# First mixer of a fp32 decoder trunk: gate and drive products from VectorE to GpSimd, and three orders of the work in its attention steps

## The chip, the cores and the metric

One core of one Trainium2 chip. The time is device microseconds of one execution; three executions of the kernel before took 1423.74, 1423.98 and 1425.97 us, median 1423.98.

## The reference

Two decoder layers on 512 tokens of width 1024, all in fp32. Each layer is a mixer, cross-attention to 256 memory tokens and a SwiGLU block, each behind an RMS norm. The change touches the mixer of layer 0 alone, which is

```python
proj = h @ w_in
x_br, y_br, q, k, v = jnp.split(proj, list(AB_SPLITS), axis=-1)
rec = rg_lru(causal_depthwise_conv(x_br, conv_w, conv_b), wa, ba, wx, bx, lam) * jax.nn.gelu(y_br)
...
att = dilated_attention(q, k, heads(v))
return jnp.concatenate([rec, att], axis=-1) @ w_out
```

and inside `rg_lru`

```python
r = jax.nn.sigmoid(block_diag_linear(x, wa, ba)); i = jax.nn.sigmoid(block_diag_linear(x, wx, bx))
log_a = -LRU_C * r * jax.nn.softplus(-lam); a = jnp.exp(log_a)
u = jnp.sqrt(-jnp.expm1(2.0 * log_a)) * (i * x)
h_t = a_t * h_{t-1} + u_t
```

`i * x` is the gate product, the product with the square root is the drive. Eight heads of width 64 attend over the 512 tokens.

## The kernel before

Activations stand transposed: 8 tiles of 128 channels x 512 tokens. Every matrix product is fp32 by three matmuls (`product`, L556, L559, L560): high part of the weight by high part of the activation, high by low, low by high. Weights arrive in **units** of 128x1024 values, 226 in the whole program, through a ring of 4 slots:

- SP issues the DMA of unit u once TensorE has begun unit u - 3 (`unit`, a wait on `s_used`);
- GpSimd makes its high part, `w_hi` (`high_part`, L512);
- VectorE subtracts to get the low part, `w_lo` (`low_part`, L1007), which overwrites the raw weights;
- TensorE waits for the low part and runs the 24 matmuls of 512 columns of the unit.

Each engine has one instruction stream, written out by hand; what stands behind a waiting instruction on its engine waits too. Nothing is reordered. `low_to(u)` on VectorE and `high(u0, u1)` on GpSimd issue all low (high) parts up to a unit at that place.

The first mixer in order: units in_x (8), in_q (4), gates (4, one per 256 channels), in_k (4), in_v (4), y0 to y7 (the branch for GeLU), 4 units for the memory's keys, and out0 (2 groups of 6). The mixer's own units are numbered from `mx_unit`; its units 0 to 7 are y0 to y7, 8 to 11 the memory's keys, and 12 onwards belong to out0.

**The recurrence.** ScalarE takes two sigmoids per tile from PSUM (`lru_r`, L1662, and `gate_i`, L1665). VectorE forms `xc = gate_i * xc` (`gated`, L1263), between the rotations of q (`qk_tile`, L1079 to L1082) and low parts. ScalarE makes the decay `lru_a` and the square root (`s_ls`). VectorE's `recur` forms the drive `lru_r * xc` (L1285) and runs the scan over the tokens (L1286), tile by tile, with the rotations of k and the low parts of in_v 3 and of y0 to y2 between. Then come the maxima of the attention's step 0 (L1331).

**The attention steps.** Twelve steps s = 0 to 11 compute scores, three steps for each pair of heads. TensorE's step is: values of an earlier pair, transposes of earlier probabilities (`mixer_turns`, L849), scores (L833), then a unit of weights (`y_half(s)` for s < 8, memory keys for s < 12, then units of out0 at s = 12 to 16). Scores of step s wait for the maxima of step s - 1. `y_half` with odd s completes two y tiles in PSUM; VectorE multiplies them by the norm (`y_tile`, L1292), and the first matmul of the next y tile in that bank waits for it (`s_y`). VectorE's step is written out in this loop:

```python
if s < STEPS + 2:
    low_to(mx_unit + s + 3)
if s in (1, 3, 5, 7):
    y_tile(s - 1)
```

preceded by the copies of transposed probabilities (L1347), the maxima, at s = 3, 6, 9, 12 the reciprocals of the denominators (L1339), the low part of a head output (`mixer_output`, L1352) and `rec`, the product with GeLU (L1296). STEPS is 12. GpSimd at s = 3, 6, 9, 12 normalises both heads of the pair, four instructions each (`normalise_pair`, L504), and at every step makes one high part, behind them. After the loop VectorE waits for the last head output and `residual` issues the low parts still missing.

## Time and profile before

| what | value |
|---|---|
| median of three runs | 1423.98 us |
| the profiled execution | 1420.2 us, span 1418.4 us |
| TensorE busy | 1349.2 us, 95% |
| VectorE busy | 771.0 us, 54% |
| ScalarE busy | 356.3 us, 25% |
| GpSimd busy | 313.3 us, 22% |
| DMA | 127.18 MB, mean 90 GB/s |

Busy shares are over the whole span; a matmul's end is modelled, so TensorE's share is an upper reading. The profile names engines PE (TensorE), PEld (its weight loads), DVE (VectorE), ACT (ScalarE), POOL (GpSimd) and SP. In a timeline row a bracket gives the idle time before the instruction and what ended it; "x2" says that two equal instructions are merged, and a length then spans both.

### The profile page before, as it was taken

How to read it: one execution, taken by the hardware profiler on the slowest of the kernel's cores; microseconds unless marked ns; L12 is line 12 of the kernel's file. 1: busy time of each engine (PE TensorE's matmuls, PEld its weight loads, DVE VectorE, ACT ScalarE, POOL GpSimd, SP SyncE). 2: the span in 40 equal slices, each digit the busy share in tenths (PEclk: the TensorE clock that was granted, in tenths of full speed). 3: DMA queues.
4: the chain of work that ended last, by engine and by line, in shares of the span. 5: the costliest groups of instructions: out<-in, count | busy, mean ns of one | idle time of the engine just before them, and what ended most of it. 6: DMA issues, size and time to landing. Idle time of an engine off the chain costs nothing.

```text
span 1418.4 us, 17415 instructions
## 1 busy us (share of the span) xinstructions
PE 1349.2 (95%) x6440; PEld 1104.4 (78%) x6440; DVE 771.0 (54%) x1147; ACT 356.3 (25%) x730; POOL 313.3 (22%) x358
## 2 busy tenths in 40 slices
PE   8999799999899999999999986799899999999997
PEld 7888577788678888888888875688678888888886
DVE  6997856436475443344436867438475443344434
ACT  4338255212342110001112235513331110001113
POOL 2222123312321212121212124312321121212120
PEclk9999899999999999999999997899999999999999
DMA  5333222222223332323233320022223332333321
GB/s 197 99 102 89 60 75 75 68 96 89 89 90 98 95 100 93 102 91 103 89 104 89 104 90 16 1 89 90 71 79 103 91 102 94 100 95 98 97 95 74
DMA packets 92418, 127.18 MB, mean 90 GB/s; under 512 B 5568, under 2 KB 58048, under 8 KB 92352
## 3 DMA queue, kind: packets, MB, share of 16 engines
q1 hardware_dynamic: 92352, 126.27, 28.0%
q8 instruction: 45, 0.74, 0.2%
q14 instruction: 21, 0.17, 0.0%
HBM read 124.15 MB, written 2.10 MB: 89 GB/s over the span
## 4 chain that ended last, share of the span: by engine, by line
PE 76%; DVE 9%; issue 6%; POOL 4%; DMA 3%; ACT 1%; SPq 0%; DVEq 0%; POOLq 0%; ACTq 0%
PE ps L556 24%; PE ps L560 24%; PE ps L559 24%; DVE w_lo L1007 2%; POOL w_hi L512 2%; DVE acc L1028 1%; DVE prob_attn L1122 1%; DMA raw<-in_w_in 1%; DMA raw<-in_xa_wkv 1%; DVE h L1047 1%; POOL prob_xattn L493 1%; POOL prob_attn L493 1%; PE ps L692 1%; DVE xc L1286 1%; POOL prob_mixer L504 1%
## 5 line engine op out<-in xcount | busy, mean ns | idle before, releaser
L1007 DVE TENSOR_TENSOR w_lo<-raw,w_hi 128x1024 fp32r<-128x1024 f32 x226 | 283.0, 1253 | 466.5 <-POOL w_hi L512 464.9
L512 POOL TENSOR_SCALAR w_hi<-raw 128x1024 fp32r<-128x1024 f32 x226 | 247.8, 1097 | 966.3 <-DMA raw<-in_w_gate_up 410.5
L556 PE MATMUL ps<-z_hi,w_hi 128*128 128x512 f32 x1040 | 409.8, 394 | 7.1 <-DVEq L1050 2.9
L560 PE MATMUL ps<-z_hi,w_lo 128*128 128x512 f32 x1040 | 405.8, 390 | 0.0
L559 PE MATMUL ps<-z_lo,w_hi 128*128 128x512 f32 x1040 | 405.6, 390 | 0.0
L556 PE MATMUL ps<-f_hi,w_hi 128*128 128x512 f32 x608 | 240.6, 396 | 3.9 <-DVE w_lo L1007 2.8
L556 PEld LDWEIGHTS ps<-z_hi,w_hi 128*128 128x128 f32 x1040 | 195.9, 188 | 54.5 <-issue 6.1
L560 PE MATMUL ps<-f_hi,w_lo 128*128 128x512 f32 x608 | 238.0, 391 | 0.0
L559 PE MATMUL ps<-f_lo,w_hi 128*128 128x512 f32 x608 | 237.9, 391 | 0.0
L559 PEld LDWEIGHTS ps<-z_lo,w_hi 128*128 128x128 f32 x1040 | 196.0, 188 | 41.8 <-issue 1.4
L560 PEld LDWEIGHTS ps<-z_hi,w_lo 128*128 128x128 f32 x1040 | 195.7, 188 | 41.0
L556 PEld LDWEIGHTS ps<-f_hi,w_hi 128*128 128x128 f32 x608 | 115.0, 189 | 29.2 <-DVE w_lo L1007 3.0
L559 PEld LDWEIGHTS ps<-f_lo,w_hi 128*128 128x128 f32 x608 | 115.0, 189 | 24.6 <-issue 1.0
L560 PEld LDWEIGHTS ps<-f_hi,w_lo 128*128 128x128 f32 x608 | 115.0, 189 | 24.3
L1769 ACT ACTIVATE ff_g<-ff_g 128x512 f32<-128x512 f32 x44 | 27.8, 632 | 347.0 <-DVE ff_g L1464 346.9
L1772 ACT ACTIVATE f_hi<-ff_u 128x512 f32 (+1 forms) x44 | 27.2, 633 | 183.4 <-DVE ff_u L1475 183.4
L1514 ACT ACTIVATE z_hi<-h,vec 128x512 fp32r<-128x512 f32 x48 | 34.8, 724 | 142.5 <-DVEq L1052 141.4
L1537 ACT ACTIVATE sq<-h 128x512 f32<-128x512 f32 x56 | 35.2, 629 | 49.0 <-DVEq L1052 23.3
L1047 DVE TENSOR_TENSOR h<-ps,h 128x512 f32<-128x512 f32 x56 | 38.5, 688 | 12.5 <-PE ps L560 11.6
L1022 DVE SCALAR_TENSOR_TENSOR z_lo<-h,vec,z_hi 128x512 fp32r<-128x512 f32 x48 | 39.6, 826 | 9.1 <-DVE h L1047 6.9
L1464 DVE TENSOR_TENSOR ff_g<-ps,rstd 128x512 f32<-128x512 f32 x44 | 30.3, 692 | 22.2 <-PE ps L560 22.1
L493 POOL TENSOR_SCALAR prob_attn<-prob_attn,stat 128x128 f32<-128x128 f32 (+1 forms) x64 | 31.7, 515 | 43.9 <-DVE stat L1137 43.9
(205 smaller groups left out, 1189.5 us busy)
## 6 DMA issues: line engine op xcount, KB each, us to landing
raw<-in_w_gate_up SPq DMA_DIRECT2D x176, 256.0 KB
raw<-in_w_down SPq DMA_DIRECT2D x44, 512.0 KB
raw<-in_w_in SPq DMA_DIRECT2D x20, 512.0 KB
raw<-in_w_out SPq DMA_DIRECT2D x20, 512.0 KB
raw<-in_xa_wkv SPq DMA_DIRECT2D x16, 512.0 KB
raw<-in_w_in SPq DMA_DIRECT2D x16, 256.0 KB
raw<-in_xa_wq SPq DMA_DIRECT2D x8, 512.0 KB
raw<-in_xa_wo SPq DMA_DIRECT2D x8, 512.0 KB
```

Of the source, the lines that this page charges most:

```text
L493: ins = pool.tensor_scalar(a["prob"][n % 3][:, c:c + w], a["prob"][n % 3][:, c:c + w], stat[:, n % 3, 4, i:i + 1], 1.0, ALU.mult, ALU.mult)
L512: pool.tensor_scalar(w_hi[:, slot], raw[:, slot], 1.0, 1.0, ALU.mult, ALU.mult).then_inc(s_hi, 1)
L556: ins = pe.matmul(o, whi, rhi, start=start, stop=False)
L559: pe.matmul(o, whi, rlo, start=False, stop=False)
L560: return pe.matmul(o, wlo, rhi, start=False, stop=stop)
L1007: dve.tensor_tensor(w_lo[:, slot], raw[:, slot], w_hi[:, slot].bitcast(F32), ALU.subtract).then_inc(s_lo, 1)
L1022: dve.scalar_tensor_tensor(z_lo[:, m, :], h[:, m, :], v(f"g_{norm}", m), z_hi[:, m, :].bitcast(F32), ALU.mult, ALU.subtract).then_inc(s_zl, 1)
L1047: ins = dve.tensor_tensor(h[:, m, :], ps[:, b, :], h[:, m, :], ALU.add)
L1464: dve.tensor_tensor(ff_g[:, p, :], ps[:, b0 + p, :], rstd[:], ALU.mult).then_inc(s_ff_gate, 1)
L1514: act.activation(dst[:, m, :], h[:, m, :], ACT.Identity, scale=v(f"g_{norm}", m)).then_inc(s_zh, 1)
L1537: act.activation(sq[:, m % 2, :], h[:, m, :], ACT.Square).then_inc(s_sq, 1)
L1769: act.activation(ff_g[:, p, :], ff_g[:, p, :], ACT.Silu).then_inc(s_ff_silu, 1)
```

## The change

- The eight gate products and the eight drive products are issued by GpSimd (`gated`, `driven`), with the same operands. ScalarE's waits on `s_gx` are unchanged; VectorE's scan waits for the new semaphore `s_drive` in place of `s_ls`.
- GpSimd's high parts of in_k, in_v and the first y units are issued between these products at written-out places.
- `normalise_pair` makes the step's high part between the first and the second head.
- On VectorE the y tile of an odd step comes ahead of that step's low part, and the low parts are issued in the loop for two steps more (s < STEPS + 4).

```diff
--- before.py
+++ after.py
@@ -272,7 +272,7 @@
         s_xch, s_xcl = sem("s_conv_hi"), sem("s_conv_lo")
         s_y_done, s_y, s_yg = sem("s_y_done"), sem("s_y_scaled"), sem("s_gelu")
         s_sp_e, s_sp = sem("s_exp_lambda"), sem("s_softplus")
-        s_gate, s_gx = sem("s_gate_i"), sem("s_gated_input")
+        s_gate, s_gx, s_drive = sem("s_gate_i"), sem("s_gated_input"), sem("s_drive")
         s_at, s_lq, s_ls = sem("s_decay"), sem("s_one_minus_a2"), sem("s_input_scale")
         s_rec, s_rech, s_recl = sem("s_rec"), sem("s_rec_hi"), sem("s_rec_lo")
         s_q0, s_v0 = sem("s_qk0"), sem("s_v0")
@@ -494,10 +494,12 @@
                                              stat[:, n % 3, 4, i:i + 1], 1.0, ALU.mult, ALU.mult)
                 ins.then_inc(a["s_prob"], 1)
 
-            def normalise_pair(p):
+            def normalise_pair(p, unit):
 
                 pool.wait_ge(mx["s_rden"], p + 1)
                 for e in range(2):
+                    if e:
+                        high(unit, unit + 1)
                     prob = mx["prob"][2 * p + e]
                     for i in range(TB):
                         c, w = mx["start"][i], P * (i + 1)
@@ -525,12 +527,34 @@
                     high_part(u, u % SLOTS)
 
             at_unit = 0
+            def gated(m):
+
+                pool.wait_ge(s_gate, m + 1)
+                pool.tensor_tensor(xc[:, m, :], gate_i[:, m % 2, :], xc[:, m, :], ALU.mult).then_inc(s_gx, 1)
+
+            def driven(m):
+
+                pool.wait_ge(s_ls, m + 1)
+                pool.tensor_tensor(lru_r[:, m, :], lru_r[:, m, :], xc[:, m, :], ALU.mult).then_inc(s_drive, 1)
+
+            first = UNIT0["gates"]
+            high(at_unit, first + 4)
+            for m in range(DB):
+                gated(m)
+                if m % 2:
+                    high(first + 4 + m // 2, first + 5 + m // 2)
+            high(first + 8, first + 11)
+            for m in range(DB):
+                driven(m)
+                if m in (5, 7):
+                    high(first + 6 + m - (m == 7), first + 7 + m - (m == 7))
             first = UNIT0["mixer"]
-            high(at_unit, first + 2)
+            high(first + 1, first + 2)
             for s in range(STEPS + 2):
                 if s % 3 == 0 and s:
-                    normalise_pair(s // 3 - 1)
-                high(first + s + 2, first + s + 3)
+                    normalise_pair(s // 3 - 1, first + s + 2)
+                else:
+                    high(first + s + 2, first + s + 3)
             at_unit = first + STEPS + 4
             for name in ("xattn0", "attn1", "xattn1"):
                 first = UNIT0[name]
@@ -1258,19 +1282,10 @@
                     dve.wait_ge(s_q0, t)
                 rotate(x_[:, n, :], x_[:, n, :], rope0, s_q0, cos_r, sin_r)
 
-            def gated(m):
-                dve.wait_ge(s_gate, m + 1)
-                dve.tensor_tensor(xc[:, m, :], gate_i[:, m % 2, :], xc[:, m, :], ALU.mult).then_inc(s_gx, 1)
-
             gates0 = UNIT0["gates"]
             for t in range(4):
                 qk_tile(t)
-                if t:
-                    gated(2 * t - 2)
-                    gated(2 * t - 1)
                 low_to(gates0 + 3 + t)
-            gated(6)
-            gated(7)
             low_to(gates0 + 7)
 
             def decay(m):
@@ -1281,8 +1296,7 @@
 
             def recur(m):
 
-                dve.wait_ge(s_ls, m + 1)
-                link(dve.tensor_tensor(lru_r[:, m, :], lru_r[:, m, :], xc[:, m, :], ALU.mult))
+                dve.wait_ge(s_drive, m + 1)
                 link(dve.tensor_tensor_scan(xc[:, m, :], lru_a[:, m, :], lru_r[:, m, :], 0.0, ALU.mult, ALU.add))
 
             def y_tile(m):
@@ -1378,10 +1392,10 @@
                 if s in (STEPS, STEPS + 1):
                     for m in range(4 * (s - STEPS), 4 * (s - STEPS) + 4):
                         rec_low(m)
-                if s < STEPS + 2:
-                    low_to(mx_unit + s + 3)
                 if s in (1, 3, 5, 7):
                     y_tile(s - 1)
+                if s < STEPS + 4:
+                    low_to(mx_unit + s + 3)
             dve.wait_ge(mx["s_o_lo"], 4)
             dve.nop().then_inc(s_free[(GROUP0["mixer"] + 1) % 2], 4)
             residual("xa0", s_done["out0"], group0=GROUP0["out0"], units=(UNIT0["out0"] + 6, UNIT0["xq0"]))
```

GpSimd from the gates to the first pair of heads, before (line 512 makes a high part, 504 normalises):

```order
L512 TENSOR_SCALAR w_hi<-raw 128x1024 x4
L374 REGISTER_ALU
L374 COMPARE_AND_BRANCH
L512 TENSOR_SCALAR w_hi<-raw 128x1024 x5
L504 TENSOR_SCALAR prob_mixer_127<-prob_mixer_127,stat_107 128x128
L504 TENSOR_SCALAR prob_mixer_127<-prob_mixer_127,stat_107 128x256
L504 TENSOR_SCALAR prob_mixer_127<-prob_mixer_127,stat_107 128x384
L504 TENSOR_SCALAR prob_mixer_127<-prob_mixer_127,stat_107 128x512
```

and now (533 is a gate product, 538 a drive product, 514 a high part, 506 normalises):

```order
L533 TENSOR_TENSOR xc<-gate_i,xc 128x512 x2
L514 TENSOR_SCALAR w_hi<-raw 128x1024
L533 TENSOR_TENSOR xc<-gate_i,xc 128x512 x2
L514 TENSOR_SCALAR w_hi<-raw 128x1024
L533 TENSOR_TENSOR xc<-gate_i,xc 128x512 x2
L514 TENSOR_SCALAR w_hi<-raw 128x1024
L533 TENSOR_TENSOR xc<-gate_i,xc 128x512 x2
L514 TENSOR_SCALAR w_hi<-raw 128x1024 x4
L538 TENSOR_TENSOR lru_r<-lru_r,xc 128x512 x6
L514 TENSOR_SCALAR w_hi<-raw 128x1024
L538 TENSOR_TENSOR lru_r<-lru_r,xc 128x512 x2
L514 TENSOR_SCALAR w_hi<-raw 128x1024 x5
```

The products stand in front of high parts of in_k (first three pairs), between in_k and in_v, and six of the drive products ahead of in_v 3.

VectorE at step 3 of the attention, before, from the reciprocals of the first pair:

```order
L1339 RECIPROCAL stat_107<-stat_107 128x8
L1007 TENSOR_TENSOR w_lo<-raw,w_hi 128x1024
L1292 TENSOR_TENSOR y_in<-ps,rstd 128x512 x2
L1347 COPY prob_t_mixer_135<-ps 128x384
L1331 ISA prob_mixer_129,stat_107<-ps,m_82 128x384
```

and now (line 1353 is the reciprocal, 1031 a low part, 1306 a y tile):

```order
L1353 RECIPROCAL stat_107<-stat_107 128x8
L1306 TENSOR_TENSOR y_in<-ps,rstd 128x512
L1031 TENSOR_TENSOR w_lo<-raw,w_hi 128x1024
L1306 TENSOR_TENSOR y_in<-ps,rstd 128x512
L1361 COPY prob_t_mixer_135<-ps 128x384
L1345 ISA prob_mixer_129,stat_107<-ps,m_82 128x384
```

The two y tiles stood together behind the low part; now one is ahead of it and one behind, and the copy of the transposed probabilities follows.

VectorE at the end of the steps, before (1300 is a recurrence tile's low part, 1352 a head output's low part, 1047 a residual tile of out0):

```order
L1300 TENSOR_TENSOR f_lo<-xc,f_hi 128x512 x4
L1007 TENSOR_TENSOR w_lo<-raw,w_hi 128x1024
L1347 COPY prob_t_mixer_142<-ps 128x384
L1352 TENSOR_TENSOR f_lo<-ps,f_hi 128x512 x2
L1007 TENSOR_TENSOR w_lo<-raw,w_hi 128x1024 x5
L1047 TENSOR_TENSOR h<-ps,h 128x512
```

and now (1314, 1366 and 1071 are the same three):

```order
L1314 TENSOR_TENSOR f_lo<-xc,f_hi 128x512 x4
L1031 TENSOR_TENSOR w_lo<-raw,w_hi 128x1024
L1361 COPY prob_t_mixer_142<-ps 128x384
L1366 TENSOR_TENSOR f_lo<-ps,f_hi 128x512
L1031 TENSOR_TENSOR w_lo<-raw,w_hi 128x1024 x2
L1366 TENSOR_TENSOR f_lo<-ps,f_hi 128x512
L1031 TENSOR_TENSOR w_lo<-raw,w_hi 128x1024 x3
L1071 TENSOR_TENSOR h<-ps,h 128x512
```

Two low parts of weights stand between the last two head outputs; before, all five came behind the last one.

## Rows read from the trace of the kernel before

**Rows 1.** the page: the chain that ended last, by engine, and the costliest GpSimd group
```profile
PE 76%; DVE 9%; issue 6%; POOL 4%; DMA 3%; ACT 1%; SPq 0%; DVEq 0%; POOLq 0%; ACTq 0%
...
L512 POOL TENSOR_SCALAR w_hi<-raw 128x1024 fp32r<-128x1024 f32 x226 | 247.8, 1097 | 966.3 <-DMA raw<-in_w_gate_up 410.5
```

**Rows 2.** TensorE by stretch: stretch and length, busy (instructions), granted clock, DMA share, GB/s
```profile
109.70:160.00 50.30, 50.26 (x224) 1.00 0.32 95
160.00:168.70 8.70, 0.10 (x1) 0.62 0.00 0
168.70:172.50 3.80, 3.79 (x10) 0.52 0.10 10
...
191.70:194.10 2.40, 0.13 (x3) 1.00 0.01 3
281.00:285.00 4.00, 4.00 (x11) 0.57 0.34 131
```

**Rows 3.** who waited for whom, 160 to 169 us; groups by form, 80 to 280 us
```profile
PE ps L833 <- DVE stat L1331: 8.6, 1, 8.6
...
L1263 DVE TENSOR_TENSOR xc<-gate_i,xc 128x512 f32<-128x512 f32 x8 | 7.0, 901 | 1.5 <-ACT gate_i L1665 1.5
```

**Rows 4.** VectorE in order of time, 131 to 169 us: start, length, instruction
```profile
131.55 1.23 DVE L1007 TENSOR_TENSOR w_lo<-raw,w_hi 128x1024 fp32r<-128x1024 f32 x1 [1.88 <-POOL w_hi L512]
...
141.28 1.95 DVE L1007 TENSOR_TENSOR w_lo<-raw,w_hi 128x1024 fp32r<-128x1024 f32 x1
143.16 0.74 DVE L1079 STREAM_SHUFFLE rope<-k 128x512 f32<-128x512 f32 x1
...
149.35 1.22 DVE L1007 TENSOR_TENSOR w_lo<-raw,w_hi 128x1024 fp32r<-128x1024 f32 x1
...
168.23 0.42 DVE L1331 CUSTOM_DVE_ANT_0 prob_mixer<-ps,m 128x256 f32<-128x256 f32 x1
```

**Rows 5.** VectorE and GpSimd where both read SBUF, and GpSimd's 128x512 alone
```profile
134.66 0.69 DVE L1285 TENSOR_TENSOR lru_r<-lru_r,xc 128x512 f32<-128x512 f32 x1
135.39 1.23 DVE L1286 TENSOR_TENSOR_SCAN xc<-lru_a,lru_r 128x512 f32<-128x512 f32 x1
135.80 1.66 POOL L512 TENSOR_SCALAR w_hi<-raw 128x1024 fp32r<-128x1024 f32 x1 [4.29 <-DMA raw<-in_w_in]
136.65 1.35 DVE L1285 TENSOR_TENSOR lru_r<-lru_r,xc 128x512 f32<-128x512 f32 x1
...
191.24 2.05 DVE L1007 TENSOR_TENSOR w_lo<-raw,w_hi 128x1024 fp32r<-128x1024 f32 x1 [5.26 <-POOL w_hi L512]
...
235.45 0.69 POOL L504 TENSOR_SCALAR prob_mixer<-prob_mixer,stat 128x512 f32<-128x512 f32 x1
```

**Rows 6.** the stops of TensorE at 192, 241 and 248 us and what stands before them
```profile
184.52 0.50 PE L556 MATMUL ps<-z_hi,w_hi 128*128 128x512 f32 x1
186.07 4.12 POOL L504 TENSOR_SCALAR prob_mixer<-prob_mixer,stat 128x128 f32<-128x128 f32 x8 [10.14 <-DVE stat L1339]
193.21 1.28 DVE L1292 TENSOR_TENSOR y_in<-ps,rstd 128x512 f32<-128x512 f32 x2
194.03 0.47 PE L556 MATMUL ps<-z_hi,w_hi 128*128 128x512 f32 x1 [2.27 <-DVE y_in L1292]
...
239.23 2.06 DVE L1007 TENSOR_TENSOR w_lo<-raw,w_hi 128x1024 fp32r<-128x1024 f32 x1 [5.26 <-POOL w_hi L512]
241.81 0.98 PE L849 MATMUL ps<-ident,prob_mixer 128*128 128x128 f32 x7 [0.84 <-DVE prob_t_mixer L1347]
...
248.87 0.50 PE L556 MATMUL ps<-f_hi,w_hi 128*128 128x512 f32 x1 [1.15 <-DVEq L1372]
```

**Rows 7.** the end of the mixer, 268 to 281 us, three engines
```profile
268.09 1.05 POOL L512 TENSOR_SCALAR w_hi<-raw 128x1024 fp32r<-128x1024 f32 x1 [5.19 <-DMA raw<-in_w_out]
...
278.74 0.69 DVE L1352 TENSOR_TENSOR f_lo<-ps,f_hi 128x512 fp32r<-128x512 f32 x1 [13.54 <-ACT f_hi L1721]
...
280.86 0.50 PE L556 MATMUL ps<-f_hi,w_hi 128*128 128x512 f32 x1 [2.79 <-DVE w_lo L1007]
```

## The prediction

> **What bounds the kernel now.** I read the chain that ended last first: 76% of it is TensorE, 9% VectorE, 6% issue, 4% GpSimd [rows 1]. So time can be won only where TensorE stands still or is slow, and only in the first mixer, which alone is edited. The table of stretches shows where that is [rows 2]. From 109.7 to 160.0 us TensorE is busy 50.26 of 50.30 us: nothing that other engines do late there costs anything as yet. From 160.0 to 168.7 it does nothing. Three shorter stops follow, of 2.27, 0.84 and 1.15 us before the matmuls at 194.03, 241.81 and 248.87 [rows 6], and one of 2.79 us before 280.86 [rows 7]. The clock comes on top: from 168.7 to 172.5 TensorE had 0.52 of its clock, from 281.0 to 285.0 it had 0.57, so mostly the lower of its two levels (1.2 of 2.4 GHz), after stops of 8.6 and 2.8 us; around the stop of 2.27 us it kept 1.00 [rows 2].
>
> Then, for each stop, who ended it. The long one is ended by a statistic of VectorE (L1331), 8.6 us [rows 3]: the maxima of step 0, which end at 168.65 (168.23 + 0.42) [rows 4]. VectorE reaches them at the end of one unbroken piece of work that begins at 131.55, when the high part of unit in_v 2 is there: low parts, the eight recurrences, four rotations of k. So a microsecond off this piece is a microsecond off the stop, up to 8.6. The stop at 191.7 is ended by y_in at 193.21+, which stands in VectorE's order behind a low part; that one waited for GpSimd, whose order was: eight normalising instructions (186.07 to 190.19), then the high part [rows 6]. At 239.23 the same pattern. The stop at 278.1 is ended by the low part of unit 16 of the mixer (out0's fifth), which VectorE issues only behind the last head output, f_lo at 278.74 [rows 7]; the high part of the unit after it had been made at 268.09.
>
> **The change, part by part.**
>
> *Gate products on GpSimd (8).* They leave VectorE between 93 and 110 us (7.0 us busy [rows 3]) and are issued by GpSimd between high parts. They may delay the high parts of in_k by a product or two; the cover is the stretch 109.7 to 160 in which TensorE never waits [rows 2]. GpSimd has room: it stood idle 966 us ahead of high parts [rows 1]. Cost and gain nil. If the cover failed, the price would be one wait of a product's length at the start of in_k.
>
> *Drive products on GpSimd (8).* This is the disputed part. VectorE loses eight products, each 0.73 us from its start to its scan's (134.66 to 135.39 [rows 5]): 8 x 0.73 = 5.8 us, all in the piece that sets the long stop. But now each scan waits for GpSimd's product, behind which stand GpSimd's high parts of in_v 3 (asked for by the low part at 141.28 [rows 4], hence VectorE waits for products 4 and 5 too) and y0 to y2. What matters is whether a product runs beside VectorE. The rows say no: GpSimd's high part at 135.80 took 1.66 us while a scan ran until 136.62, and the VectorE product asked for at 136.65 took 1.35 instead of 0.69, until the high part was over; the low part at 191.24 took 2.05 against 1.22 for that at 149.35 [rows 4, 5]. Instructions of the two engines that both read SBUF take turns, whole instruction by whole instruction. So a product moved to GpSimd still costs VectorE's chain its length.
>
> Its length is in no row. Lower end: GpSimd's one-input operation on the same 128x512, 0.69 us [rows 5]. A high part moves 128x1024 in, as many elements as the two inputs of a product, and takes 1.05 undisturbed (268.09 [rows 7]; mean of all 226, waits included, 1.097 [rows 1]). Upper end: twice that, 2.1. I take 1.05, since the number of elements read is the same.
> - eight products: 8 x 1.05 = +8.4
> - taken off VectorE: -5.8
> - one product beside a shuffle of 0.74, which reads one tile [rows 4]: -0.7
> - a GpSimd instruction that has stood waiting ended 0.84 after the scan, not 1.05 (136.62 to 137.46) [rows 5]; about five of eight wait so: -1.0
> - sum: **+0.9 us**; at the lower end 5.5 - 5.8 - 1.7 = -2.0, at the upper 16.8 - 5.8 - 1.7 = +9.3.
>
> So the largest edit should win nothing: the long stop and the slow clock behind it stay. The low part of y0, done at 150.57 before [rows 4], gets some 5 us later and makes TensorE wait about a microsecond at 154.4; this only moves idle time forward, since TensorE would wait for the maxima anyway.
>
> The Trainium skill (SBUF — State Buffer, Who interferes with whom) says that a VectorE instruction with two SBUF inputs and a GpSimd one that reads SBUF exclude each other for the whole instruction; by that rule the trace agrees (1.35 for 0.69). The Trainium skill (GPSIMD Engine Reference, Elementwise — side-by-side cycle accounting) speaks against the move: 4497 ns for a two-input operation on 2048 elements, so 1.12 us for 512 as an estimate, with which the sum would be +1.5; no row here has a product on GpSimd.
>
> *y tiles ahead of low parts, step 3.* y_in of tile 2 needs only the first half of y_half(3), which began at 184.52 [rows 6]: 12 of its matmuls at the pace of 224 in 50.3 us [rows 2] are 2.7 us, so 187.2; VectorE is free since 186.0, when GpSimd begins to normalise. So it is ready at 188 and tile 3 at about 191, before TensorE needs them at 191.76 (194.03 less 2.27) and half a unit later. **-2.3 us** [rows 6]. Behind it, the low part of that step comes at about 189.2 instead of 191.24: the high part now follows four normalisings (half of 4.12 us) instead of eight. Late next: the second head's probabilities, by 1.05 us plus a low part's turn, until about 192.3; TensorE turns them at step 5, after 197. Covered. At steps 1, 5 and 7 the low part waits for a y tile that follows half a unit; it is needed a unit later or more.
>
> *High part between heads, steps 6, 9, 12.* At step 9 the low part starts some 2 us before its 239.23, by half of such a normalising. VectorE's copy, maxima and low parts follow 2 us earlier; the 0.84 us stop at 241.81 goes, and of the 1.15 before 248.87 some 0.4, since there memory_keys itself must end before mk is copied. **-1.2 us** (ends: -0.8 if only the first goes, -2.0 if both). At step 6 TensorE did not wait; at step 12 neither.
>
> *Low parts at steps 14 and 15 (the bound is now STEPS + 4).* Units 16 and 17 get their low parts at about 265 and 270, behind high parts of which the second is there at 269.1 [rows 7] and the first a step earlier. The last two turns of TensorE's steps then don't wait: **-2.8 us** [rows 7], and without that stop the clock should not fall: 4.0 us at 0.57 would be 2.3, **-1.7 us** [rows 2]. Late next: f_lo of the last head, 279.43, wanted only by unit 17, 5.5 us later. Covered.
>
> No DMA is added; SP's waits are on TensorE's progress and move with it.
>
> Sum: 0.9 - 2.3 - 1.2 - 2.8 - 1.7 = **-7.1 us**. The profiled execution took 1420.2 us (span 1418.4), so 1413.1 for such a one. The median of the runs is 3.8 us above it; I take the difference over to it: 1423.98 - 7.1 = 1416.9. A measurement of this kernel can tell about 0.2% (2.8 us) from no change.
>
> **The rivals.**
>
> *The products do run beside VectorE.* Then 5.8 us come off the chain, the long stop shrinks to 2.8, and the slow clock (3.8 us at 0.52, 1.8 us) may go or stay, since 2.79 brought it and 2.27 did not: -5.8 - 0.9 - 8.0 = -14.7, 1409.3. For it: no two-input GpSimd operation has been seen. Against: the turns in [rows 5]. 12%.
>
> *The stops won later come back.* The microseconds of the y tiles and heads meet the next wait (scores behind maxima, copies behind turned heads), and only the end of the mixer is won: 0.9 - 2.8 - 1.7 = -3.6, 1420.4. For it: behind the maxima the exponentials, GeLU and the recurrence's product follow one another on two engines before the next low part. Against: VectorE was idle 5.26 us just ahead of the low parts at 191.24 and 239.23 [rows 5, 6]. 18%.
>
> *The product is dear (the other side).* Each scan waits for one, and taking turns puts every microsecond of eight products into the 131 to 168 piece. The late gains of 8.0 are eaten when the product takes 0.9 + 8 (p - 1.05) = 8.0, p = 1.94; at the upper end of 2.1 the time is 1425.3, and at 2.5 it is 1428.5. From 2.3 on it is measurably slower. For it: GpSimd's per-element work with two inputs is unseen. Against: one-input work runs at 1.0 ns an element. 10%.
>
> **How the numbers follow.** Forecast 60%, with its own range 1413 (product 0.69, both small stops) to 1422.6 (product 1.5, clock still falls). The range of 8 in 10 takes in most of the first rival: 1408 to 1423. Faster by over 0.2% (below 1421.1): 57 of the 60, the 12, and half of the 18: 0.78. Within: 0.14. Slower: the worse part of the last rival, 0.08.
>
> **What would show it.** Right: product on GpSimd near 1.05 to 1.25 us and longer when a scan runs; the stop before step 1's scores still 8 to 10 us, with a granted clock near half after it; no stop for y_in near 192; full clock through out0. Wrong: that stop shrunk below 4 us (products overlap) or grown past 14 (dear product); a new stop of over 1 us between 190 and 250; a fall of the clock in out0; any part of the kernel after 300 us that changes by more than the profile repeats.

## The result and the profile after

The change runs in 1415.64 us (median of 6 runs, 1411.88 to 1418.62), the kernel before beside it in 1423.06 (6 runs, 1418.67 to 1425.97). The ratio is 0.9948, with a 95% interval of 0.9924 to 0.9972: 7.4 us less, between 4.0 and 10.8. A second set of 5 runs gave 0.9952 [0.9939, 0.9966], 6.8 us less. The forecast was 7.1 less, 1416.9.

The profiled execution of the change took 1417.91 us (span 1416.1), only 2.3 us below the profiled one of before. The profiled one of before was a quick execution (1420.2 beside a median of 1423.06), and the two profiles differ in places that the change doesn't touch; how much of each difference is the change's is worked out below by stretches.

The page of the change: busy time by engine, and the chain that ended last.

```profile
PE 1348.0 (95%) x6440; PEld 1103.1 (78%) x6440; DVE 777.5 (55%) x1131; ACT 356.1 (25%) x730; POOL 348.1 (25%) x374
...
PE 78%; DVE 8%; issue 6%; POOL 4%; DMA 2%; ACT 1%; SPq 0%; DVEq 0%; POOLq 0%; ACTq 0%
```

TensorE's share of the chain went from 76 to 78%, VectorE's from 9 to 8% [rows 1]. Sixteen instructions left VectorE and came to GpSimd. What they cost there stands in the groups of GpSimd by form, 80 to 170 us (busy us, mean ns; idle time before), and in the shortest, median and longest drive product:

```profile
L538 POOL TENSOR_TENSOR lru_r<-lru_r,xc 128x512 f32<-128x512 f32 x8 | 15.7, 2000 | 0.0
L533 POOL TENSOR_TENSOR xc<-gate_i,xc 128x512 f32<-128x512 f32 x8 | 13.8, 1744 | 3.0 <-ACT gate_i L1679 3.0
```

```profile
L538 POOL TENSOR_TENSOR lru_r<-lru_r,xc x8: 1285/2213/2291, 131.5 to 146.0; 128x512 f32<-128x512 f32 x8
```

A product undisturbed takes 1.285 us. The usual one takes 2.2, most of it spent waiting for a scan to end. VectorE in order of time shows the same from the other side (start, length, instruction, idle time before):

```profile
131.60 2.30 DVE L1031 TENSOR_TENSOR w_lo<-raw,w_hi 128x1024 fp32r<-128x1024 f32 x1 [1.61 <-POOL w_hi L514]
133.83 8.84 DVE L1300 TENSOR_TENSOR_SCAN xc<-lru_a,lru_r 128x512 f32<-128x512 f32 x4
144.87 2.23 DVE L1031 TENSOR_TENSOR w_lo<-raw,w_hi 128x1024 fp32r<-128x1024 f32 x1 [2.21 <-POOL w_hi L514]
...
148.73 1.52 DVE L1105 TENSOR_TENSOR rope<-rope,sin_r 128x512 f32<-128x512 f32 x1
150.29 1.42 DVE L1106 TENSOR_TENSOR k<-rope,rope 128x512 f32<-128x512 f32 x1
...
154.98 1.22 DVE L1031 TENSOR_TENSOR w_lo<-raw,w_hi 128x1024 fp32r<-128x1024 f32 x1
156.12 4.99 DVE L1300 TENSOR_TENSOR_SCAN xc<-lru_a,lru_r 128x512 f32<-128x512 f32 x4
...
170.44 0.42 DVE L1345 CUSTOM_DVE_ANT_0 prob_mixer<-ps,m 128x256 f32<-128x256 f32 x1
```

The first four scans take 8.84 us, the last four, with no product beside them, 4.99. One scan, the product issued while it ran, and the next scan:

```profile
136.19 2.14 DVE L1300 TENSOR_TENSOR_SCAN xc<-lru_a,lru_r 128x512 f32<-128x512 f32 x1
137.20 2.22 POOL L538 TENSOR_TENSOR lru_r<-lru_r,xc 128x512 f32<-128x512 f32 x1
...
138.36 2.14 DVE L1300 TENSOR_TENSOR_SCAN xc<-lru_a,lru_r 128x512 f32<-128x512 f32 x1
```

They end at 138.33, 139.42 and 140.50, each some 1.09 us behind the one before. So the two engines take turns, as in [rows 5], but not for the whole of an instruction: a scan and a product together take 2.17 us where one after the other would be 1.23 + 1.285 = 2.52, so 0.35 us of each pair is hidden.

The piece from the low part of in_v 2 to the maxima of step 0 was 37.10 us (131.55 to 168.65, [rows 4]) and is 39.26 now (131.60 to 170.86): +2.2. VectorE issues eight instructions fewer in it and ends later. By the starts in both profiles, the second four scans with what belonged to them are 3.6 us shorter, since their products were ready; the first four are 0.2 longer; the low part at 131.60 costs 1.1 more (2.30 instead of 1.23, [rows 4]) and that at 144.87 0.3; VectorE stands idle 2.2 us ahead of the latter, whose high part GpSimd makes behind six products; and the first two rotations of k take 1.8 more (steps of 1.52 and 1.42 instead of 0.69), beside high parts that the products have pushed back. The Trainium skill (SBUF — State Buffer, Who interferes with whom) has the two engines exclude each other for the whole instruction. Here that holds for all but the 0.35 us of a pair.

TensorE's stops in the change, in order of time (start, length, matmul, idle time before and what ended it):

```profile
109.84 0.50 PE L580 MATMUL ps<-z_hi,w_hi 128*128 128x512 f32 x1 [0.83 <-ACTq L1682]
...
156.25 0.60 PE L580 MATMUL ps<-z_hi,w_hi 128*128 128x512 f32 x1 [1.75 <-DVE w_lo L1031]
...
170.92 1.65 PE L857 MATMUL ps<-k,q 64*128 64x384 f32 x4 [7.31 <-DVE stat L1345]
...
248.28 0.50 PE L580 MATMUL ps<-f_hi,w_hi 128*128 128x512 f32 x1 [0.65 <-DVEq L1386]
```

Of the stops in [rows 6] those at 194.03 and 241.81 have no counterpart, that at 248.87 is down from 1.15 to 0.65, and that at 280.86 [rows 7] is gone: the mixer's last matmuls run straight into its unit 16 at 277.41. New is the one before 156.25, for the low part of y0. The table of TensorE's stretches of the change (stretch and length, busy, granted clock, DMA share, GB/s) answers [rows 2]:

```profile
109.80:156.20 46.40, 44.67 (x200) 1.00 0.31 91
156.30:161.00 4.70, 4.70 (x14) 0.64 0.37 113
...
171.00:175.00 4.00, 4.00 (x10) 0.50 0.13 18
...
191.00:260.00 69.00, 68.30 (x467) 1.00 0.24 77
260.00:300.00 40.00, 40.00 (x213) 1.00 0.24 82
```

From 260 to 300 us TensorE was busy 40.00 of 40.00 us at the full clock; before it was 37.21 of 40.00:

```profile
260.00:300.00 40.00, 37.21 (x194) 0.96 0.22 76
```

**The stretches.** Three marks divide the mixer, each the start of a matmul: in_k's first, step 1's first scores (behind the long stop), out0's first unit; a fourth is the first stop of the cross-attention behind it. The lengths between them, worked out from the starts in each profile (us), take out what differed before 109 us and behind 370 us:

```
kernel                         in_k to    scores    out0 to   in_k to
                               scores     to out0   attention attention
before [rows 6]                 58.97      80.16     119.71    258.84
before, second profile          59.05      80.78     119.75    259.58
change                          61.08      77.36     115.26    253.70
change, second profile          61.13      76.86     115.24    253.23
products back on VectorE        59.24      76.59     115.25    251.08
products alone                  61.10      82.77     119.67    263.54
gate products alone, with rest  59.32      76.78     115.26    251.36
y tile order alone              58.64      78.82     119.66    257.12
head order alone                59.08      77.40     118.09    254.57
low bound alone                 60.87      80.73     115.25    256.85
drive with one input            55.74      77.56     115.27    248.57
```

The change against before, by the means of two profiles each: +2.1, -3.4, -4.5, together -5.7. The predicted terms were +0.9 for the first, -3.5 (2.3 and 1.2) for the second, -4.5 (2.8 and 1.7) for the third.

### The profile page after: what moved, and what is told of

Same layout as the page of the kernel before. It is cut to its first block, busy times and chain, and to the rows that moved or that the text cites. A ratio compares the mean times of both kernels' runs of the same rounds, so it can differ in the third digit from the quotient of the medians.

```text
span 1416.1 us, 17405 instructions
## 1 busy us (share of the span) xinstructions
PE 1348.0 (95%) x6440; PEld 1103.1 (78%) x6440; DVE 777.5 (55%) x1131; ACT 356.1 (25%) x730; POOL 348.1 (25%) x374
## 4 chain that ended last, share of the span: by engine, by line
PE 78%; DVE 8%; issue 6%; POOL 4%; DMA 2%; ACT 1%; SPq 0%; DVEq 0%; POOLq 0%; ACTq 0%
PE ps L580 25%; PE ps L583 24%; PE ps L584 24%; DVE w_lo L1031 1%; POOL w_hi L514 1%; DVE acc L1052 1%; DVE prob_attn L1146 1%; DVE h L1071 1%; PE ps L716 1%; DMA raw<-in_xa_wkv 1%; POOL lru_r L538 1%; POOL prob_xattn L493 1%; POOL prob_attn L493 1%; PE ps L684 1%; DVE z_lo L1046 1%
## 5 line engine op out<-in xcount | busy, mean ns | idle before, releaser
L514 POOL TENSOR_SCALAR w_hi<-raw 128x1024 fp32r<-128x1024 f32 x226 | 251.4, 1112 | 926.2 <-DMA raw<-in_w_gate_up 411.5
L1783 ACT ACTIVATE ff_g<-ff_g 128x512 f32<-128x512 f32 x44 | 27.8, 632 | 348.2 <-DVE ff_g L1478 348.2
```

Source lines behind the costliest of these rows:

```text
L514: pool.tensor_scalar(w_hi[:, slot], raw[:, slot], 1.0, 1.0, ALU.mult, ALU.mult).then_inc(s_hi, 1)
L1783: act.activation(ff_g[:, p, :], ff_g[:, p, :], ACT.Silu).then_inc(s_ff_silu, 1)
```

## The experiments

Each kernel was timed beside the kernel before on one chip; ratios have their 95% interval. In microseconds they are taken on that set's median of before (1424.22, 1422.6 and 1424.36).

**1. Both products back on VectorE; all that the change does later is kept.**

```diff
-                dve.wait_ge(s_drive, m + 1)
+                dve.wait_ge(s_ls, m + 1)
+                link(dve.tensor_tensor(lru_r[:, m, :], lru_r[:, m, :], xc[:, m, :], ALU.mult))
...
+                if t:
+                    gated(2 * t - 2)
+                    gated(2 * t - 1)
```

> The change without its first part: gate and drive products back on VectorE, the head order, y tile order and the two further low parts kept. Theory A (a GpSimd product and VectorE's scans take turns at SBUF, so the products cost): the scores of step 1 start near 168.7 us as before (170.9 in the change), the stop of 1.75 us before the first y unit and the low clock behind it go, and the time is 2.5 to 3.5 us below the change, about 10 us below before. Rival B (the products are neutral): same as the change, 7 us below before. Rival C (they help): slower than the change.

Measured: 1415.03 us, 0.9933 [0.9917, 0.9950], 9.5 us less than before. In its profile the first stretch is back at 59.2 and the other two are the change's. So the later parts carry the whole gain, and the products give a part of it back: 2.4 us by the length from in_k to the attention (253.5, the mean of the change's two profiles, against 251.1), 2.1 to 2.7 by the ratios, which were taken on different chips and whose intervals overlap.

**2. The products alone, on the kernel before.**

```diff
-            def gated(m):
-                dve.wait_ge(s_gate, m + 1)
-                dve.tensor_tensor(xc[:, m, :], gate_i[:, m % 2, :], xc[:, m, :], ALU.mult).then_inc(s_gx, 1)
...
+            def driven(m):
+                pool.wait_ge(s_ls, m + 1)
+                pool.tensor_tensor(lru_r[:, m, :], lru_r[:, m, :], xc[:, m, :], ALU.mult).then_inc(s_drive, 1)
```

> The kernel before with only the sixteen products moved to GpSimd. Theory A: the scores of step 1 at about 171 us, a new stop of 1 to 2 us before the first y unit, and a time 2.5 to 3.5 us above before. Rival B: no difference. Rival C: several us below before, with the stop before step 1 shrunk from 8.6 towards 3 us.

Measured: 1423.59 us (12 runs), 0.9992 [0.9981, 1.0002]: no change that can be told. The first stretch is 61.10, as in the change. The stop for the low part of y0 is there too, and the y_in stop stays. TensorE's stops in it:

```profile
155.73 0.79 PE L577 MATMUL ps<-z_hi,w_hi 128*128 128x512 f32 x1 [1.77 <-DVE w_lo L1028]
...
170.39 1.65 PE L854 MATMUL ps<-k,q 64*128 64x384 f32 x4 [7.32 <-DVE stat L1342]
...
196.69 0.76 PE L577 MATMUL ps<-z_hi,w_hi 128*128 128x512 f32 x1 [2.24 <-DVE y_in L1303]
```

The expectation of 2.5 to 3.5 us above before failed. The first stretch alone would make this kernel 2.1 us slower, and the other half of this edit, the gate products, gives some 0.8 back (experiment 4). That leaves +1.3, and the interval of the runs ends at +0.3: the last microsecond stays open. The profile can't tell, since it is that of the slowest of the 12 executions (1427.17 us), and its long middle stretch (82.77) has a slower clock behind the y_in stop, which neither profile of before has:

```profile
196.69:203.00 6.31, 6.31 (x21) 0.73 0.28 86
```

**3. The drive product with one input.** Each drive product is an operation of the same size with one input, so the product with xc is left out of the computation.

```diff
-                pool.tensor_tensor(lru_r[:, m, :], lru_r[:, m, :], xc[:, m, :], ALU.mult).then_inc(s_drive, 1)
+                pool.tensor_scalar(lru_r[:, m, :], lru_r[:, m, :], 1.0, 1.0, ALU.mult, ALU.mult).then_inc(s_drive, 1)
```

> The changed kernel with the drive product on GpSimd replaced by a one-input copy of the same 128x512 shape (the product with xc is left out of the computation). Theory A (the length of the product sits in VectorE's chain, 1.29 us against 0.69): eight times 0.6 us come off, the scores of step 1 start near 166 us instead of 170.9. Rival D (what costs is the hand-over between the engines, a wait per scan, not the length): they start at 170 or later.

Measured: 1411.01 us, 0.9898 [0.9881, 0.9914]. Its drive line (shortest, median, longest) and the long stop:

```profile
L538 POOL TENSOR_SCALAR lru_r<-lru_r x8: 615/1516/1586, 130.6 to 140.3; 128x512 f32<-128x512 f32 x8
```

```profile
164.66 1.65 PE L857 MATMUL ps<-k,q 64*128 64x384 f32 x4 [5.40 <-DVE stat L1345]
```

Undisturbed, the operation is 0.67 us shorter (615 against 1285 ns). Eight times that is 5.4, and the first stretch is 5.3 shorter than the change's (55.74 against 61.08). So a microsecond more of a product on GpSimd is a microsecond more of VectorE's chain, as the prediction's formula had it, and no mere cost of handing over. The hidden part is the same in both: here a scan and an operation take 1.48 us (1.23 + 0.615 = 1.85 one after the other). (The timed distance to the change, by the ratios of two chips, is 7.7 us; the 2.4 beyond the first stretch are not found in the profiles.)

**4. The gate products on GpSimd, the drive products on VectorE**, beside the change and the kernel before once more, on the same chip.

```diff
-            high(first + 8, first + 11)
-            for m in range(DB):
-                driven(m)
-                if m in (5, 7):
-                    high(first + 6 + m - (m == 7), first + 7 + m - (m == 7))
+            high(first + 8, first + 13)
...
-                dve.wait_ge(s_drive, m + 1)
+                dve.wait_ge(s_ls, m + 1)
+                link(dve.tensor_tensor(lru_r[:, m, :], lru_r[:, m, :], xc[:, m, :], ALU.mult))
```

> The changed kernel with the drive products back on VectorE and the gate products left on GpSimd. Theory G (the gate products on GpSimd help: on VectorE they hold up ScalarE's sigmoids, and TensorE starts in_k 2.0 us late instead of 0.83; the drive products cost): stop before in_k at 0.83, scores of step 1 near 168, time 1 to 3 us below both the change and e1. Rival H (gate products neutral): same as e1.

> The changed kernel again, on the same chip as its variants. Every theory: 6 to 9 us below before. Its profile shows whether the stop of 1.75 us before the first y unit, the low clock behind it and the late scores of step 1 (170.9) are steady or chance.

> The kernel before once more, for a second profile. Theory F (the first profile was a lucky one: its median is 4 us above it, and other profiles show 2.10 us instead of 0.70 at the cross-attention and a low clock behind stops of about 2 us): this profile shows at least one of these, or the stop of 2 us instead of 0.83 us before in_k at about 109 us. Rival: the same stops to 0.1 us.

Measured: the gate products alone 1412.96 us, 0.9928 [0.9914, 0.9941]; the change 1415.13, 0.9952 [0.9939, 0.9966]. On one chip, the drive products cost 2.2 us by the medians and 3.4 by the ratios, and by the profiles 1.8 (61.13 against 59.32). All five executions of the one are shorter than all five of the other (at most 1414.17, at least 1414.46).

The second profile of the kernel before brought what the prediction had missed. Its TensorE waited 1.88 us ahead of in_k, where the first profile had 0.83, and ScalarE's rows say why (start, length, instruction; in brackets its wait). TensorE's row follows:

```profile
97.47 0.69 ACT L1665 ACTIVATE gate_i<-ps,vec 128x512 f32<-128x512 f32 x1 [0.16 <-DVE xc L1263]
...
103.23 0.69 ACT L1665 ACTIVATE gate_i<-ps,vec 128x512 f32<-128x512 f32 x1 [0.49 <-DVE xc L1263]
...
109.13 0.69 ACT L1665 ACTIVATE gate_i<-ps,vec 128x512 f32<-128x512 f32 x1 [0.94 <-DVE xc L1263]
```

```profile
111.09 0.50 PE L556 MATMUL ps<-z_hi,w_hi 128*128 128x512 f32 x1 [1.88 <-ACTq L1668]
```

gate_i has two buffers, and ScalarE may fill one only when the product has read it. In this execution VectorE was late with the products, each time by more, and ScalarE handed it on to TensorE. In the first profile of before it was the other way round: VectorE waited for gate_i, 1.5 us in all [rows 3], and the stop was 0.83. Of the seven profiles with the gate products on VectorE five have the long form (1.88 to 2.06 us), two the short one; of the seven with them on GpSimd none has it, all show 0.83. From the first gate_i to in_k's first matmul it is 16.93 us in the short form (92.81 to 109.74) and 17.99 in the long one (93.10 to 111.09). So the gate products on GpSimd save 1.1 us in about five executions of seven, 0.8 on average; in_k's first matmul starts at 110.1 in the mean of the one seven profiles and at 109.0 in that of the other. The runs can't settle it: by the ratios this kernel and experiment 1 are 0.7 us apart (0.9928 and 0.9933), with intervals that overlap. Five of seven is a small count. What decides the form lies ahead of the gates: VectorE began its first rotation of q 7.1 to 7.2 us ahead of the first gate_i in the two short profiles, 3.8 to 4.6 us ahead in the five long ones. What makes it late there stays open.

**5. The y tile ahead of the low part, alone.**

```diff
-                if s < STEPS + 2:
-                    low_to(mx_unit + s + 3)
                 if s in (1, 3, 5, 7):
                     y_tile(s - 1)
+                if s < STEPS + 2:
+                    low_to(mx_unit + s + 3)
```

> The kernel before with only the y tile of an odd step ahead of the low part. Theory A: the stop of 2.2 us before the y unit of step 4 becomes shorter but may not go, since the head order is unchanged and tile 3 still stands behind the low part at 191; 1 to 2.3 us are won, and up to 1.8 more where the low clock followed that stop; all other stops stay. Rival I (the stop moves to the next step): stops in steps 4 to 6 sum to the same.

Measured: 1419.0 us (11 runs), 0.9969 [0.9959, 0.9980], 4.4 less. The stop at 192 is gone; those of 0.83 at 240.68, 1.20 at 247.78 and 2.79 at 279.77 stay. The middle stretch is 1.7 shorter than the mean of before.

**6. The high part between the heads, alone.**

```diff
-            def normalise_pair(p):
+            def normalise_pair(p, unit):
...
+                    if e:
+                        high(unit, unit + 1)
...
-                    normalise_pair(s // 3 - 1)
-                high(first + s + 2, first + s + 3)
+                    normalise_pair(s // 3 - 1, first + s + 2)
+                else:
+                    high(first + s + 2, first + s + 3)
```

> The kernel before with only the step's high part between the two heads. Theory A: the low part of step 3 starts 2 us earlier, so the stop of 2.2 us in step 4 becomes about 0.2, that of 0.8 in step 11 goes and that before out0 shrinks from 1.2 to about 0.7: 2.5 to 3.5 us won. Rival: the second head's probabilities come late and TensorE waits for them in steps 5, 8, 11 or 14.

Measured: 1416.95 us, 0.9956 [0.9941, 0.9972], 6.3 less. This edit alone removes the stop at 241 and the one at 192 too: VectorE in its profile, behind the earlier high part:

```profile
190.12 1.39 DVE L1010 TENSOR_TENSOR w_lo<-raw,w_hi 128x1024 fp32r<-128x1024 f32 x1 [3.21 <-POOL w_hi L514]
191.43 1.28 DVE L1295 TENSOR_TENSOR y_in<-ps,rstd 128x512 f32<-128x512 f32 x2
```

The low part comes 1.1 us earlier and is 0.66 shorter than before (1.39 against 2.05, [rows 5]), since a short normalising instruction runs beside it and not another high part (GpSimd at 190.06 to 190.43 here, at 191.17 to 192.22 before), and y_in starts 1.8 earlier. So the two reorderings earn the same 2.3 us at step 3. The middle stretch is 3.1 shorter here and 1.7 shorter in experiment 5, and with both, in experiment 1, 3.9. Yet experiment 1 has no stop fewer than this kernel between the scores and out0 (one, 0.66 us in both), and its whole lead of 0.8 us is there when step 2's scores start, 8.54 us behind step 1's against 9.35 here. It is the clock behind the long stop, 20 us of it in experiment 1 and then here:

```profile
169.10:189.10 20.00, 20.00 (x81) 0.89 0.26 79
```

```profile
168.51:188.51 20.00, 20.00 (x77) 0.85 0.24 70
```

The second profile of before had 0.87 there, that of experiment 5 had 0.86. So the y tile order adds nothing to the head order.

The end of the mixer holds a lesson on the clock. This kernel still has the stop of 2.79 us:

```profile
277.90 0.50 PE L559 MATMUL ps<-f_hi,w_hi 128*128 128x512 f32 x1 [2.79 <-DVE w_lo L1010]
```

```profile
260.00:300.00 40.00, 37.21 (x201) 1.00 0.24 79
```

Behind the same stop the clock stayed at 1.00, where both profiles of before show 0.96 over these 40 us. The third stretch is 118.09 instead of 119.7: 1.6 us, which is the predicted price of the clock (1.7) by itself. Of the five profiles with this stop it is the only one that kept the clock.

**7. The low parts of two more steps in the loop, alone.**

```diff
-                if s < STEPS + 2:
+                if s < STEPS + 4:
                     low_to(mx_unit + s + 3)
```

> The kernel before with only the two further low parts in the loop (units 16 and 17 at steps 14 and 15). Theory A: the stop of 2.79 us before unit 16 and the clock of about 0.57 behind it go, 4.5 us are won (2.8 + 1.7). Rival: the clock stays low for another reason and 2.8 us are won.

Measured: 1416.49 us, 0.9949 [0.9933, 0.9965], 7.3 less. The third stretch is 115.25: 4.5 shorter, the predicted 2.8 and 1.7 to a tenth. The timed gain is larger than that by 2.8, about the half-width of its interval (2.3) and a little more; the profile doesn't show where it would be. Its first stretch is 1.9 longer than before's (60.87), and the part as such has no effect there. It is the long form of the gate stop once more, this time with a slower clock behind it:

```profile
109.50:135.00 25.50, 24.18 (x99) 0.93 0.30 83
```

Seven hundredths of 25.5 us are 1.8, about the 1.9. In the long forms of experiment 1, of experiment 5 and of the second profile of before the clock stayed at 1.00.

**8. The chain of the long stop in another order.** All the above leaves the largest stop where it is: step 1's scores wait for the maxima of step 0, and behind its first four scans VectorE puts four more, four rotations and four low parts ahead of those maxima. In three kernels only one scan, one rotation and two low parts stay ahead of them; the rest is spread over steps 0 to 5: on experiment 1 (products on VectorE), on experiment 4 (gate products on GpSimd), and on the change itself. The edit of the second and third:

```diff
             qk_tile(4)
-            qk_tile(5)
+            recur(4)
             low_to(gates0 + 13)
-            for m in range(4, DB):
-                recur(m)
-            low_to(gates0 + 13)
-            qk_tile(6)
-            low_to(gates0 + 14)
-            qk_tile(7)
             mx_unit = UNIT0["mixer"]
-            low_to(mx_unit + 3)
...
                     mixer_maxima(s)
+                if s == 0:
+                    low_to(mx_unit + 2)
+                    recur(5)
+                    recur(6)
+                if s == 1:
+                    recur(7)
+                if s == 2:
+                    qk_tile(5)
+                if s == 4:
+                    qk_tile(6)
+                if s == 5:
+                    qk_tile(7)
```

The first has qk_tile(5) at step 1, not 2.

> Products on VectorE as in e1, and the long stop attacked itself: on VectorE only the recurrences 0 to 4, one rotation of k and the low part of y0 stand ahead of the maxima of step 0; recurrences 5 to 7 and the other rotations follow in steps 0, 1, 4 and 5. Theory A (the long stop is VectorE's order alone): the 8.6 us stop and the low clock behind it (1.8 us) go, and 8 to 10 us more come off than in e1, so 16 to 20 us below before. Rival E (the moved work only moves the stop to steps 1 to 5): 0 to 4 us below e1.

> e8 with the gate products on GpSimd and the fifth rotation moved from step 1 to step 2. Theory G: stop before in_k 0.83 us instead of 2.06, the stop of 1.40 us before y unit 2 gone, so 2 to 3 us below e8, about 23 us below before. Rival: no difference to e8.

> e10 with the drive products on GpSimd as well, as in the change, but VectorE's new order. Theory A (a product on GpSimd costs only where VectorE's chain sets the end): scans 0 to 4 are late by about 3 us, the low part of the first y unit comes after TensorE wants it, a stop of 1 to 2 us at 154 us and perhaps the low clock behind it remain: 1 to 3 us slower than e10. Rival: no slower, since the chain now has several us to spare.

Measured:

```
products on VectorE        1403.15 us  0.9849 [0.9834, 0.9863]
gate products on GpSimd    1401.61 us  0.9855 [0.9840, 0.9870]
both on GpSimd             1403.93 us  0.9856 [0.9836, 0.9875]
```

All three are 20.5 to 21.5 us faster than the kernel before and 13 to 15 faster than the change. Against the kernels that differ in this edit alone, the reordering wins 12.0 us (experiment 1), 10.4 (experiment 4) and 13 to 14 (the change). In the first one stop is left between in_k and out0, for a y_in that follows the rotation at step 1:

```profile
170.24 0.47 PE L569 MATMUL ps<-z_hi,w_hi 128*128 128x512 f32 x1 [1.40 <-DVE y_in L1305]
```

In the second there is none. Its VectorE now reaches the maxima of step 0 at 153.22 and waits for TensorE there, not the other way round:

```profile
153.22 0.29 DVE L1335 CUSTOM_DVE_ANT_0 prob_mixer<-ps,m 128x128 f32<-128x128 f32 x1 [4.51 <-PE ps L853]
```

```profile
109.00:233.00 124.00, 123.51 (x683) 1.00 0.28 86
```

That is 123.51 of 124.00 us busy at the full clock. From in_k to the attention it takes 240.1 us (108.36 to 348.47), 19.1 less than before and 11.3 less than experiment 4. In the third the drive products on GpSimd leave a stop of 0.32 us at 154.37, and that length is 240.5: where VectorE's chain has slack, the same two microseconds of turns cost 0.4. The runs don't tell these versions apart: the second was expected 2 to 3 us below the first and is not (0.9855 and 0.9849), though its profile is 3.0 shorter from in_k to the attention; the third was expected 1 to 3 above the second and is not either (0.9856), so there the rival held.

## Why the prediction was right

**The sum.** Predicted -7.1, measured -7.4 and -6.8 in two sets of runs. By the stretches and the gate stop: +2.1 - 3.4 - 4.5 - 0.8 = -6.6. Two terms were off, one up and one down, and they nearly cancel: that the sum met the time this well is in part luck. The stretches also leave out a difference behind the third stop of the cross-attention, +1.7 us in the profiles (below), for which the prediction had no term; with it the profiles give -4.9, which is just inside the intervals of both sets.

**Drive products: the mechanism right, the size off.** The prediction took 1.05 us for a product by the number of elements read, between bounds of 0.69 and 2.1; it takes 1.285. Put into its own formula (0.24 more, eight times) the term is +2.8; the profiles show +2.1, and the one-input experiment moves the chain by 5.3 where the lengths say 5.4. The term of -1.0 for waiting products had the right cause: one ended 1.09 us behind the scan, not 1.285. A scan behind a product gains likewise (1.08 instead of 1.23), for which there was no term. And the cost comes in elsewhere than the formula says, mostly as VectorE's wait for the high part behind six products (2.2 us). The estimate worked out from the Trainium skill (GPSIMD Engine Reference, Elementwise — side-by-side cycle accounting), 1.12 us and so +1.5, was nearer than 1.05 and still short of the measured 1.285. That the long stop stays (7.31 and 8.91 us), and that the largest edit wins nothing, was right: alone it measures 0.9992 [0.9981, 1.0002].

**The low part of y0** was to come 5 us later, with a microsecond of waiting at 154.4 that only moves idle time forward. It started 5.6 later (154.98 against 149.35), and the stop was 1.75. It cost nothing, as said: in the second profile of the change the clock kept 1.00 behind it (154 to 163 us), in the first it fell to 0.64, and the scores start 61.1 us behind in_k in both, because the long stop takes up the difference (7.31 and 8.91 us).

**Gate products: the step that failed.** "Cost and gain nil" named TensorE's cover from 109.7 on and GpSimd's idle time, but not who waits for the product in the stretch before: ScalarE, through the two buffers of gate_i, and TensorE behind it. The rows shown [rows 3] had VectorE waiting for gate_i there, and one profile was taken for the rule. It is the rarer of the two forms seen. The term is about -0.8 by the profiles, and more where the slower clock follows the long form, as it did in two of those five (1.8 us each).

**y tiles and heads:** -3.5 predicted for both, -3.9 measured without the products and -3.4 (mean of two) with them. The assignment was off: the head order does not only reach step 9 but also undoes the stop at step 3, so that by the stops it earns all of it alone and the y tile order adds nothing to it (experiment 6); what the stretches differ by beyond that is the clock behind the long stop. No wait came in their place: between 190 and 250 us the one stop is 0.65.

**Low parts at steps 14 and 15:** -4.5 predicted, -4.5 in every profile that has the edit and a full clock. The clock's 1.7 of it is a matter of chance: the head order alone kept the clock behind the same stop.

**The rivals.** That products run beside VectorE is excluded, but for the 0.35 us of a pair, by the turns of scans and products and by the one-input experiment. That the stops won come back is excluded by the middle stretch. The dear product needed 1.94 us and is 1.285.

**After 300 us** the prediction asked for nothing that changes. One thing does: the third stop of the cross-attention is 2.10 us in both profiles of the change and 0.70 and 0.42 in those of before.

```profile
374.08 1.18 PE L699 MATMUL ps<-ident,prob_xattn 128*128 128x128 f32 x8 [2.10 <-POOL prob_xattn L493]
```

```profile
379.14 1.09 PE L675 MATMUL ps<-ident,prob_xattn 128*128 128x128 f32 x8 [0.70 <-POOL prob_xattn L493]
```

The stop itself costs nothing. From the matmul behind the first of the three stops to that behind the third it is 10.5 to 10.6 us in all fourteen profiles. What differs is the clock. Before, it fell behind the second stop, where TensorE then worked longer and waited less, and was full behind the third:

```profile
374.22:377.02 2.80, 2.80 (x10) 0.50 0.01 3
379.12:383.12 4.00, 3.98 (x18) 1.00 0.00 0
```

In the change it held behind the second and fell behind the third, where TensorE works without a pause:

```profile
369.18:371.98 2.80, 2.79 (x12) 1.00 0.01 3
374.08:378.08 4.00, 4.00 (x13) 0.61 0.00 0
```

From there to TensorE's next stop it is 27.8 to 28.0 us in six profiles (both of before, each of the later parts alone, the fastest version) and 29.5 to 29.8 in eight (both of the change, the products alone, experiment 1 and the others): 1.7 us. By the prediction's own signs this speaks against it. No single part of the change goes with the dearer form. Whether the kernel or chance decides between the two stays open; two profiles of the same kernel agreed both times.

It is one reason why the first two profiles differ by 2.3 us only. It may also be part of why the three later parts alone gain 4.4, 6.3 and 7.3, together 18.0, and jointly 9.5: experiment 1 has the dearer form and they have not (1.7), 2.3 are counted twice at step 3, and the clock at the end is won by the head order and by the low parts both (1.6). That is 5.6 of the 8.5. The rest lies within the four intervals, of 1.5 to 2.4 us each way, and is not explained.

## What to carry to other kernels

Moving an operation with two inputs to GpSimd takes it off VectorE's count but not off its time: where both read SBUF they take turns, so on a chain that sets the end the move costs up to the difference of the two engines' lengths (here eight times 1.285 against 0.73 us, 4.4, of which 2.1 were measured), and off such a chain next to nothing (0.4 in the last version of experiment 8). Look for what stands ahead of the awaited instruction without being needed by it: taking the maxima ahead of scans and rotations won another 10 to 14 us, more than all the parts of the change together. And ask for whom a product frees a buffer: with two buffers the engine that fills them can be the one that waits, in some executions and not in others.

## What the runs showed of the hardware

- A product of two 128x512 tiles takes 1.285 us on GpSimd, the same operation with one input 0.615 (shortest of eight each). A VectorE scan beside it takes turns with it: a scan (1.23 us alone) and a product come every 2.17 us, 0.35 less than their sum.
- The granted clock behind a stop of some two microseconds differs between executions: behind 2.79 us it was 0.57 over four microseconds in the kernel before and stayed at 1.00 in experiment 6; behind 1.75 it fell to 0.64 in one profile of the change and stayed at 1.00 behind 1.82 in the other; behind the long form of the gate stop it was 0.93 from 109.5 to 135 us in experiment 7 (stop of 1.92) and in the first version of experiment 8 (2.06), and 1.00 in experiment 1 (1.92), in experiment 5 (1.94) and in the second profile of before (1.88); behind the y_in stop of 2.24 it fell to 0.73 over 6.3 us in experiment 2 and stayed at 1.00 behind 2.27 and 2.24 in the two profiles of before. Behind the stops of 7.3 to 8.9 us it was 0.50 to 0.55 for four microseconds each time. One such fall costs 1.6 to 1.8 us where no other engine is waited for, and nothing where TensorE would have stood idle anyway (the second stop of the cross-attention before). One profile against one profile is uncertain by these microseconds, and so is a length between two marks.
